# U gathers issued eighteen indices ahead of the V gathers, in place of sixteen, in a streaming encoder step

## The chip, the core and the metric

One core of one Trainium2 chip runs the whole program in one launch. The metric is the device time of an execution in microseconds (us), lower is better. The times below are of the kernel before the change; one more execution was recorded by the hardware profiler, and all rows come from that one.

## What is computed

One layer of a hybrid encoder for 1024 prompt rows and 32 sample rows of width 1024: a norm, a projection, four mLSTM heads beside eight sliding-window attention heads, an output projection, and then the part that this change touches, a product-key expert layer (PEER). For each row and each of eight heads, 16 of 16384 experts are chosen; the row is multiplied with the 16 chosen rows of the table `expert_u`, and 16 chosen rows of `expert_v` are added up with the weights that follow:

```python
idx = jnp.take_along_axis(cidx, sel, axis=-1)
g = jax.nn.softmax(top.astype(jnp.float32), axis=-1).astype(xb.dtype)
u = jnp.take(expert_u, idx, axis=0)
a = jax.nn.gelu(jnp.einsum('thkd,td->thk', u, xb), approximate=False)
ve = jnp.take(expert_v, idx, axis=0)
return jnp.einsum('thk,thkd->td', g * a, ve)
```

Everything is fp32. An expert row is 4 KB, and each (row, head) pair needs 16 of each table.

## The kernel before

The expert layer is cut into 33 subtiles of 32 rows (32 for the prompt, one for the sample), and a subtile into two groups of four heads: 66 groups (`GROUPS`). In a group the 128 partitions hold 32 rows times four heads, and `TOPK` = 16 indices follow one another. For each index one indirect DMA gathers 128 rows of `expert_u` (512 KB), another 128 rows of `expert_v`. Numbered through all groups, index n runs from 0 to 1055 in both streams; U[n] and V[n] below are these gathers. Index n = 32q + r has place r in subtile q.

**Buffers.** `ring` holds fourteen buffers, seven for U (`U_AT`) and seven for V (`V_AT`). U[n] may be gathered once VectorE is done with U[n-7] (`u_free`), V[n] once TensorE is done with V[n-7] (`v_free`).

**GpSimd** issues all gathers from one queue in one fixed order: sixteen U gathers, then pairs U[n+16], V[n] (lines 600 to 606), and at the end sixteen V gathers without partners. It waits at each gather for the free buffer (lines 581 and 593), so whatever stands behind a waiting gather waits too, of the other stream as well. The first U gather of a group also waits for the group's indices (`topk_done`).

**VectorE** takes the U stream. For U[n] it multiplies the gathered rows with the subtile's row in PSUM, `h2p`, and sums (line 1273). After a group's sixteen products ScalarE makes the gelu, and VectorE's `weigh` turns them into weights `wk` (lines 1207 to 1219); for a group in the first half of a subtile this is written behind the first product of the next group. Between the products stand pieces of the index search of a later group and the vector steps of the next tile's mixing part.

**TensorE** takes the V stream: eight matmuls for each V[n] (line 1675), weights from `wk`, sums in `acc`. Between them stand the matmuls of the next tile's mixing part and of the projection, at places that tables of numbers set. TensorE at V[t] and VectorE at U[t+16] are in the same step of these tables.

**Where the two must meet.** First, V[32q] and V[32q+16] need their group's `wk`, the former written behind product U[32q+16]. Second, `h2p` has one buffer: once in a subtile, ahead of V[32q+15], TensorE copies the rows of subtile q+1 into it (`spread_rows`, line 1628). It waits for the last product of the subtile, U[32q+31], and VectorE waits for it ahead of U[32q+32]. This handover comes 32 times in the program.

Of the kernel before, what the change touches and what calls it, by code (L numbers as in the profile page):

```python
# [28 lines left out]
PH, NK, TOPK = 8, 128, 16  # L29
# [18 lines left out]

SUB = 32
QD = D // 4  # L50
NU = 7
NV = 7
U_AT = [0, 1, 2, 3, 4, 5, 13]
# [2 lines left out]
GROUPS = 2 * (SEQ // SUB + 1)  # L56
# [119 lines left out]
def stored(b, n):  # L176

    return 16 * sum(x == b for x in UNIT_PO[:n])


def program(nc, x_prompt, x_sample, cache_k, cache_v, st_c, st_n, st_m, norm_mix_w, w_in, if_bias, mnorm_w, sinks,
# [15 lines left out]
    with ExitStack() as ctx:  # L197
        def sb(name, shape, dt=F32):
            return ctx.enter_context(nc.sbuf_tensor(name, shape, dt))

        def sem(name):
            return ctx.enter_context(nc.semaphore(name))
# [5 lines left out]
        wq_s = weights[:, DC * D:].rearrange("p (k c) -> p k c", k=DC)  # L208
        ring = sb("ring", [P, NU + NV, D])
        pj = sb("pj", [P, PJ])  # L210
# [93 lines left out]
        acc = ctx.enter_context(nc.psum_tensor("acc", [P, D], F32))  # L304
        sums = [acc[:, b * 512:b * 512 + QD] for b in range(2)]
        pbank = [acc[:, c % 2 * 512:c % 2 * 512 + PC[c][1]] for c in range(NC_)]
# [32 lines left out]
        topk_done, h2p_set = sem("topk_done"), sem("h2p_set")  # L339
        u_in = [sem(f"u_in{i}") for i in range(NU)]  # L340
        v_in = [sem(f"v_in{i}") for i in range(NV)]
# [216 lines left out]
        def _(pool):  # L558
# [16 lines left out]
            def gather_u(g, k):  # L575

                n = TOPK * g + k
                if k == 0:
                    pool.wait_ge(topk_done, g + 1)
                if n >= NU:  # L580
                    pool.wait_ge(u_free, n - NU + 1)
                elif n == 4:
                    pool.wait_ge(query_ready, 3)
                elif n == 6:
                    pool.wait_ge(proj_out[4], stored(4, len(UNITS)))
                pool.indirect_dma_start(ring[:, U_AT[n % NU], :], None, u_d,  # L586
                                        bass.IndirectOffsetOnAxis(ap=idx[:, g % 4, k:k + 1], axis=0)).then_inc(u_in[n % NU], 16)

# [8 lines left out]
                pool.indirect_dma_start(ring[:, V_AT[n % NV], :], None, v_d,  # L597
                                        bass.IndirectOffsetOnAxis(ap=idx[:, g % 4, k:k + 1], axis=0)).then_inc(v_in[n % NV], 16)

            for k in range(TOPK):  # L600
                gather_u(0, k)
            for g in range(GROUPS):
                for k in range(TOPK):
                    if g + 1 < GROUPS:
                        gather_u(g + 1, k)
                    gather_v(g, k)


# [288 lines left out]
        def _(dve):  # L897
# [330 lines left out]
            def add_rows(q):  # L1228
# [4 lines left out]
                for j in range(4):  # L1233
                    cols = slice(j * QD, (j + 1) * QD)
                    V.tensor_tensor(xt[m % 2][r, cols], xt[m % 2][r, cols], sums[q % 2][j * SUB:(j + 1) * SUB, :], ALU.add)  # L1235
# [80 lines left out]
        def _(pe):  # L1316
# [341 lines left out]
            for g in range(-1, GROUPS):  # L1658
                for k in range(TOPK):
# [5 lines left out]
                    if g >= 0 and t > 0:  # L1665
# [6 lines left out]
                        for n in (0, 1) if t == 1 else (t,):  # L1672
                            pe.wait_ge(v_in[n % NV], 16 * (n // NV + 1))
                            for j in range(4):
                                last = T.matmul(sums[g // 2 % 2][j * SUB:(j + 1) * SUB, :], wk[:, n // FEW % 5, n % FEW, :], ring[:, V_AT[n % NV], j * QD:(j + 1) * QD],  # L1675
                                                start=g % 2 == 0 and n % TOPK == 0, stop=g % 2 == 1 and k == TOPK - 1)
# [58 lines left out]
```

## Time and profile before

| what | value |
|---|---|
| median of 3 runs | 3383.86 us (3382.38 to 3389.47) |
| profiled execution | 3354.33 us |
| its span, first to last instruction | 3352.6 us |
| gathers | 2112, 512 KB each |
| mean TensorE clock granted | 0.740 |

The profile has a page of totals, a table of who waited for whom, tables of busy time in stretches of the span, and a timeline of instructions in order. Times are us from the start of the span. In all of them L586 is a U gather, L597 a V gather, L1273 a product on U, L1675 a matmul on V. A GpSimd instruction of these two lines is the making of the gather's descriptors; the transfer comes after it. `remote`, as the releaser of a wait, means that the profile did not find the instruction that ended it. In the chain that ended last, the page gives PE 31%, issue 16%, POOL 14%, DVE 13% and DMA 10%.

### The profile page before, as it was taken

What the parts mean: (1) busy time and instruction counts of PE and PEld (TensorE: products, weight loads), DVE (VectorE), ACT (ScalarE), POOL (GpSimd) and SP (SyncE); (2) the same over time, 40 slices, a digit from 0 to 9 for tenths busy, and PEclk for the clock granted to TensorE, in tenths of its full rate; (3) what the DMA queues carried; (4) which work ended last, traced back from release to release, by engine and by line L of the source; (5) the groups of instructions that cost most, each with busy time, mean ns of one, the idle gap of its engine ahead of it and who ended that gap; (6) DMA issues with size and microseconds to landing.
All of it is one profiled execution on the core that took longest, in us unless ns stands there. A gap on an engine that the chain in (4) does not pass through costs nothing.

```text
span 3352.6 us, 42363 instructions
## 1 busy us (share of the span) xinstructions
PE 2349.4 (70%) x15147; PEld 1174.5 (35%) x15147; DVE 2147.1 (64%) x5579; ACT 535.9 (16%) x1059; POOL 1992.9 (59%) x2128
## 2 busy tenths in 40 slices
PE   8995775667667888877857765668567765675545
PEld 4652352335233533334534432325223431221111
DVE  1257757776676656657577667676676676766653
ACT  2211111211121221112121111111111111210001
POOL 0036666666666566665666666666666666666665
PEclk9996796678566988987867776678676875566555
DMA  6479999999999999999999999999999999999998
GB/s 229 149 277 405 358 349 375 362 373 349 375 357 381 368 402 408 408 400 357 362 353 365 366 369 363 360 372 351 376 361 374 364 353 377 359 359 362 368 368 325
DMA packets 348955, 1197.59 MB, mean 357 GB/s; under 512 B 37760, under 2 KB 54408, under 8 KB 346952
## 3 DMA queue, kind: packets, MB, share of 16 engines
q0 software_dynamic: 304128, 1107.43, 87.8%
q1 hardware_dynamic: 44616, 87.45, 7.1%
q8 instruction: 119, 1.95, 0.2%
q14 instruction: 92, 0.75, 0.1%
HBM read 1180.69 MB, written 14.15 MB: 356 GB/s over the span
## 4 chain that ended last, share of the span: by engine, by line
PE 31%; issue 16%; POOL 14%; DVE 13%; DMA 10%; another core or an unknown queue 9%; DVEq 5%; ACT 1%; ACTq 0%; SPq 0%; POOLq 0%
PE mx L1574 9%; PE acc L1675 7%; POOL ring L597 7%; POOL ring L586 7%; DVE ring L1273 6%; DMA ring<-in_peer_v_dram,idx 4%; PE mx L1385 3%; DMA ring<-in_peer_u_dram,idx 3%; DVEq L1145 2%; PE acc L1361 2%; PE mx L1585 2%; PE mx L1556 1%; DMA weights<-in_w_in_dram 1%; PE h2p L1628 1%
## 5 line engine op out<-in xcount | busy, mean ns | idle before, releaser
L1273 DVE SCALAR_TENSOR_TENSOR ring<-ring,h2p 128x1024 f32<-128x1024 f32 x1056 | 1272.2, 1214 | 551.7 <-DMA ring<-in_peer_u_dram,idx 267.5
L1675 PE MATMUL acc<-ring,wk 128*32 128x256 f32 x8448 | 1030.7, 507 | 684.6 <-DMA ring<-in_peer_v_dram,idx 317.5
L597 POOL DMA_INDIRECT ring<-in_peer_v_dram,idx x1056 | 995.3, 942 | 790.6 <-remote 369.4
L586 POOL DMA_INDIRECT ring<-in_peer_u_dram,idx x1056 | 995.8, 943 | 554.7 <-issue 302.4
L1675 PEld LDWEIGHTS acc<-ring,wk 128*32 128x32 f32 x8448 | 316.5, 129 | 1316.5 <-issue 776.9
L1574 PE MATMUL mx<-reg,weights 128*128 128x128 f32 x1792 | 275.3, 309 | 42.4 <-issue 42.1
L1574 PEld LDWEIGHTS mx<-reg,weights 128*128 128x128 f32 x1792 | 245.8, 216 | 101.5 <-issue 101.1
L1556 PE MATMUL mx<-weights,reg 128*128 128x512 f32 (+1 forms) x256 | 138.6, 668 | 1.9 <-DVEq L1246 1.1
L1385 PE MATMUL mx<-weights 128*128 128x512 f32 (+1 forms) x288 | 132.4, 604 | 2.2 <-issue 1.4
L1628 PE MATMUL h2p<-ch,ident 32*32 32x512 f32 x528 | 104.4, 798 | 31.2 <-issue 20.2
L828 ACT ACTIVATE gl<-dots 128x16 f32<-128x16 f32 x66 | 14.2, 216 | 537.8 <-issue 368.5
L1585 PE MATMUL mx<-kT,pj 128*32 128x128 f32 x1040 | 69.5, 316 | 36.0 <-issue 30.7
L788 ACT COPY pj<-mx 128x512 f32<-128x512 f32 x32 | 18.7, 586 | 446.2 <-PE mx L1574 234.7
L1273 DVE DVE_READ_ACCUMULATOR ring<-ring,h2p 128x1 f32 x1056 | 86.8, 82 | 0.0
L828 ACT ACT_TABLE_LOAD x66 | 84.7, 1283 | 7.1 <-issue 1.7
L822 ACT ACT_TABLE_LOAD x61 | 78.3, 1283 | 44.2 <-issue 20.8
L1385 PEld LDWEIGHTS mx<-weights 128*128 128x128 f32 x288 | 55.6, 204 | 67.7 <-issue 61.2
L1235 DVE TENSOR_TENSOR xt<-xt,acc 32x256 f32<-32x256 f32 x132 | 55.1, 417 | 24.0 <-PE acc L1675 21.9
L1556 PEld LDWEIGHTS mx<-weights,reg 128*128 128x128 f32 (+1 forms) x256 | 45.5, 196 | 69.1 <-issue 66.7
L1219 DVE TENSOR_TENSOR wk<-rept,gl 128x128 f32<-128x128 f32 x264 | 65.5, 289 | 5.8 <-issue 0.5
L1585 PEld LDWEIGHTS mx<-kT,pj 128*32 128x32 f32 x1040 | 49.9, 125 | 54.6 <-issue 48.8
L1385 PE MATMUL mx<-weights,reg 128*128 128x512 f32 (+1 forms) x96 | 49.8, 670 | 22.6 <-DMA weights<-in_w_in_dram 18.4
(311 smaller groups left out, 2425.6 us busy)
## 6 DMA issues: line engine op xcount, KB each, us to landing
ring<-in_peer_u_dram,idx POOLq DMA_INDIRECT x1056
ring<-in_peer_v_dram,idx POOLq DMA_INDIRECT x1056
weights<-in_peer_w_q_dram SPq DMA_DIRECT2D x7, 2048.0 KB
weights<-in_w_in_dram SPq DMA_DIRECT2D x5, 2048.0 KB, 18.2
weights<-in_w_in_dram SPq DMA_DIRECT2D x10, 1024.0 KB
ring<-in_peer_w_q_dram SPq DMA_DIRECT2D x8, 1024.0 KB, 6.1
xt<-in_x_prompt_dram SPq DMA_DIRECT2D x8, 512.0 KB
ring<-in_w_out_dram SPq DMA_DIRECT2D x2, 2048.0 KB, 13.6
```

The costliest lines, as they stand in the source:

```text
L586: pool.indirect_dma_start(ring[:, U_AT[n % NU], :], None, u_d, bass.IndirectOffsetOnAxis(ap=idx[:, g % 4, k:k + 1], axis=0)).then_inc(u_in ...
L597: pool.indirect_dma_start(ring[:, V_AT[n % NV], :], None, v_d, bass.IndirectOffsetOnAxis(ap=idx[:, g % 4, k:k + 1], axis=0)).then_inc(v_in ...
L822: S.activation(ew[:, :], top[:, g % 3, :], ACT.Exp, bias=ntop[:, g % 3:g % 3 + 1], accum_out=ez[:, 0:1])
L828: S.activation(gl[:, :], dots[:, g % 2, :], ACT.Gelu)
L1145: dve.drain()
L1273: V.scalar_tensor_tensor(ring[:, U_AT[n % NU], :], ring[:, U_AT[n % NU], :], 1.0, h2p[:, :], ALU.mult, ALU.mult, accum_out=dots[:, (g + 1) ...
L1385: last = T.matmul(bank, hT1_again[i][:, 4 * half + k, :], wpiece[(2 * p + half) % 3][:, k, 0:w], start=half + k == 0, stop=half == 1 and k ...
L1556: last = T.matmul(mx[0:n, 2 + half, :], t8[:, k, 0:n], w, start=k == 0, stop=k == DC - 1)
L1574: last = T.matmul(mx[:, i // 4, i % 4 * P:i % 4 * P + n], w, t8[:, k, 0:n], start=k == 0, stop=k == DC - 1)
L1585: last = T.matmul(mx[q:q + SUB, i, col:col + NK], qT[:, c, i * SUB:(i + 1) * SUB], kT[:, c % 2, :], start=True, stop=True)
L1628: last = T.matmul(h2p[j * SUB:(j + 1) * SUB, cols], ident[r, r], ch[m % 2][r, cols], start=True, stop=True)
L1675: last = T.matmul(sums[g // 2 % 2][j * SUB:(j + 1) * SUB, :], wk[:, n // FEW % 5, n % FEW, :], ring[:, V_AT[n % NV], j * QD:(j + 1) * QD], ...
```

## The change

The lead of the U stream over the V stream in GpSimd's order becomes a constant, `U_AHEAD = 18`. Eighteen U gathers go first, then pairs U[n+18], V[n], and the last eighteen V gathers have no partner. The waits of each gather are the same as before, and so are the buffers and the programs of all other engines.

```diff
+U_AHEAD = 18
...
-            for k in range(TOPK):
-                gather_u(0, k)
+            for n in range(U_AHEAD):
+                gather_u(n // TOPK, n % TOPK)
             for g in range(GROUPS):
                 for k in range(TOPK):
-                    if g + 1 < GROUPS:
-                        gather_u(g + 1, k)
+                    n = TOPK * g + k + U_AHEAD
+                    if n < TOPK * GROUPS:
+                        gather_u(n // TOPK, n % TOPK)
                     gather_v(g, k)
```

GpSimd's queue at the first V gather, before: the rows are U[7] to U[15], U[16], V[0], U[17], V[1]; `topk_done` is the wait for the next group's indices.

```order
L586 DMA ring<-in_peer_u_dram,idx 128x1024 [waits u_free] x9
L586 DMA ring<-in_peer_u_dram,idx 128x1024 [waits u_free,topk_done]
L597 DMA ring<-in_peer_v_dram,idx 128x1024
L586 DMA ring<-in_peer_u_dram,idx 128x1024 [waits u_free]
L597 DMA ring<-in_peer_v_dram,idx 128x1024
```

The same place in the changed kernel, whose lines are one further down:

```order
L587 DMA ring<-in_peer_u_dram,idx 128x1024 [waits u_free] x9
L587 DMA ring<-in_peer_u_dram,idx 128x1024 [waits u_free,topk_done]
L587 DMA ring<-in_peer_u_dram,idx 128x1024 [waits u_free] x2
L598 DMA ring<-in_peer_v_dram,idx 128x1024
L587 DMA ring<-in_peer_u_dram,idx 128x1024 [waits u_free]
L598 DMA ring<-in_peer_v_dram,idx 128x1024
```

U[17] and U[18] have moved ahead of V[0], so V[0] has two gathers more in front of it, and from there on each V[n] stands right behind U[n+18].

GpSimd's queue at the end, before:

```order
L597 DMA ring<-in_peer_v_dram,idx 128x1024
L586 DMA ring<-in_peer_u_dram,idx 128x1024
L597 DMA ring<-in_peer_v_dram,idx 128x1024
L586 DMA ring<-in_peer_u_dram,idx 128x1024
L597 DMA ring<-in_peer_v_dram,idx 128x1024 x17
```

and in the changed kernel:

```order
L598 DMA ring<-in_peer_v_dram,idx 128x1024
L587 DMA ring<-in_peer_u_dram,idx 128x1024
L598 DMA ring<-in_peer_v_dram,idx 128x1024
L587 DMA ring<-in_peer_u_dram,idx 128x1024
L598 DMA ring<-in_peer_v_dram,idx 128x1024 x19
```

The last U gather now stands ahead of V[1037] where it stood ahead of V[1039]: nineteen V gathers follow it in place of seventeen.

## Rows read from the trace of the kernel before

**Rows 1.** The page: busy time of the engines, then the gathers' DMA queue.

```profile
PE 2349.4 (70%) x15147; PEld 1174.5 (35%) x15147; DVE 2147.1 (64%) x5579; ACT 535.9 (16%) x1059; POOL 1992.9 (59%) x2128
...
q0 software_dynamic: 304128, 1107.43, 87.8%
```

**Rows 2.** Table by stretch: length, busy us of engines, granted clock, DMA share, GB/s.

```profile
1200.00:1400.00 200.00, 163.03 (x863) 67.13 (x864) 126.24 (x327) 27.48 (x42) 127.13 (x135) 0.91 1.03 407
...
3000.00:3200.00 200.00, 110.04 (x726) 33.85 (x725) 133.43 (x347) 21.17 (x34) 130.67 (x139) 0.63 0.98 364
```

**Rows 3.** Waits of GpSimd: who waited for whom, us, times, longest.

```profile
POOL ring L597 <- remote: 369.4, 201, 3.6
...
POOL ring L597 <- PE acc L1675: 181.1, 127, 6.7
POOL ring L586 <- DVE ring L1273: 62.0, 79, 9.7
```

**Rows 4.** Waits of TensorE and VectorE at V and U, same table.

```profile
PE acc L1675 <- DMA ring<-in_peer_v_dram,idx: 317.5, 184, 7.9
...
DVE ring L1273 <- DMA ring<-in_peer_u_dram,idx: 267.5, 185, 4.8
...
DVE ring L1273 <- PE h2p L1628: 72.2, 12, 15.2
...
PE acc L1675 <- DVEq L1215: 51.6, 12, 10.8
```

**Rows 5.** Timeline of GpSimd at one handover: start, us, instruction, idle before.

```profile
3143.73 0.94 POOL L597 DMA_INDIRECT ring<-in_peer_v_dram,idx  x1 [0.30 <-issue]
3144.97 0.94 POOL L586 DMA_INDIRECT ring<-in_peer_u_dram,idx  x1 [0.30 <-issue]
3146.22 0.94 POOL L597 DMA_INDIRECT ring<-in_peer_v_dram,idx  x1 [0.30 <-issue]
...
3151.50 0.93 POOL L597 DMA_INDIRECT ring<-in_peer_v_dram,idx  x1 [3.10 <-PE acc L1675]
```

**Rows 6.** VectorE at the same handover: the first product of the new subtile.

```profile
3151.17 1.22 DVE L1273 SCALAR_TENSOR_TENSOR ring<-ring,h2p 128x1024 f32<-128x1024 f32 x1 [11.77 <-remote]
```

**Rows 7.** TensorE behind the same handover.

```profile
3151.07 4.09 PE L1675 MATMUL acc<-ring,wk 128*32 128x256 f32 x40 [0.39 <-issue]
3156.16 0.64 PE L1675 MATMUL acc<-ring,wk 128*32 128x256 f32 x8 [1.00 <-DMA ring<-in_peer_v_dram,idx]
```

**Rows 8.** Timeline of GpSimd at an earlier handover.

```profile
2961.36 0.94 POOL L597 DMA_INDIRECT ring<-in_peer_v_dram,idx  x1 [1.97 <-PE acc L1675]
```

**Rows 9.** VectorE at that earlier handover.

```profile
2964.69 1.22 DVE L1273 SCALAR_TENSOR_TENSOR ring<-ring,h2p 128x1024 f32<-128x1024 f32 x1 [2.74 <-PE h2p L1628]
2965.84 0.08 DVE L1273 DVE_READ_ACCUMULATOR ring<-ring,h2p 128x1 f32 x1
```

**Rows 10.** TensorE at a V gather whose weights come late.

```profile
2258.96 1.08 PE L1675 MATMUL acc<-ring,wk 128*32 128x256 f32 x8 [10.75 <-DVEq L1215]
```

**Rows 11.** VectorE ahead of those weights.

```profile
2242.07 1.22 DVE L1273 SCALAR_TENSOR_TENSOR ring<-ring,h2p 128x1024 f32<-128x1024 f32 x1
...
2254.30 0.69 DVE L1123 COPY reg<-mx 128x512 f32<-128x512 f32 x1 [11.01 <-remote]
2255.11 1.22 DVE L1273 SCALAR_TENSOR_TENSOR ring<-ring,h2p 128x1024 f32<-128x1024 f32 x1
```

**Rows 12.** Timeline of GpSimd at the start: V[0], V[4], V[5].

```profile
228.67 0.93 POOL L597 DMA_INDIRECT ring<-in_peer_v_dram,idx  x1 [0.30 <-issue]
...
241.76 0.94 POOL L597 DMA_INDIRECT ring<-in_peer_v_dram,idx  x1 [3.47 <-DMA proj_scratch<-ring]
...
250.95 0.94 POOL L597 DMA_INDIRECT ring<-in_peer_v_dram,idx  x1 [7.00 <-DMA proj_scratch<-ring]
```

**Rows 13.** Timeline at the start and the end: first matmul on V, last V gather.

```profile
247.76 1.93 PE L1675 MATMUL acc<-ring,wk 128*32 128x256 f32 x32
...
3338.08 0.93 POOL L597 DMA_INDIRECT ring<-in_peer_v_dram,idx  x1 [0.30 <-issue]
```

## The prediction, made before the changed kernel ran

> **What bounds the kernel now.** I read the page first. No engine is full: TensorE is busy for 70% of the span, VectorE for 64%, GpSimd for 59%, and the gathers' DMA queue fills 87.8% of sixteen engines [rows 1]. The table by stretch says more about the DMA: its share is 0.98 in a late stretch at 364 GB/s, but in another stretch, at a similar share, it moves 407 GB/s [rows 2]. So a share near one is not the queue at its best rate; there is about a tenth left, and it is lost somewhere in the supply of gathers.
>
> The timeline of GpSimd shows the supply. Where nothing holds it, a gather goes out every 1.24 us (3144.97 less 3143.73) [rows 5]. 2112 gathers at 1.24 us are 2619 us. From the first V gather at 228.67 [rows 12] to the last at 3338.08 [rows 13] pass 3109 us. What GpSimd waits for is in its table of waits: 369.4 + 181.1 = 550.5 us ahead of V gathers, in 328 waits, and 62.0 us ahead of U gathers, in 79 waits [rows 3]. Of each wait some 0.3 us is there in any case, as between any two gathers. The V waits carry two names, `remote` and the matmul on V; both are the wait for a free V buffer, since no other wait stands in the code there after the first seven. So the fixed order of the two streams is mostly held by TensorE, and hardly ever by VectorE.
>
> Last I read what the two consumers wait for [rows 4]. TensorE waits 184 times, 317.5 us, for a V gather to land; VectorE 185 times, 267.5 us, for a U gather. TensorE waits 12 times, 51.6 us, for weights, and VectorE 12 times, 72.2 us, for the new rows in `h2p`.
>
> **What the change does.** It adds and removes no instruction: 1056 gathers of each kind go out before and after, with the same waits. It moves each U gather two places ahead in relation to the V gathers, which is two pairs, 4 x 1.24 = 5.0 us where nothing holds the queue. Only waits can change.
>
> *Gain in the middle.* When GpSimd stands at V[n] for a free buffer, two more U gathers are already out. VectorE may then go on for two products more. That is worth something only where TensorE then waits for VectorE. There are 12 such waits for weights, 51.6 us [rows 4]. The one I looked into is the longest: TensorE idles 10.75 us until 2258.96 [rows 10]. In that time VectorE has done a product at 2242.07, then stood 11.01 us, and the instruction that it stood at is the copy of the next tile's transposed rows, which TensorE makes [rows 11]. Its next product starts at 2255.11 without any idle time for a landing. So VectorE was late for the weights because of the mixing part, not because of U. I take the gain here at nothing; its bounds are zero and 51.6 us.
>
> *Cost at the handover.* At the handover VectorE has finished U[32q+31] and TensorE is at V[32q+15]. The seven U buffers allow U[32q+38] and no more until the product on U[32q+32] is done. Before, V[32q+21] and V[32q+22] stand ahead of U[32q+39] in the queue, so V[32q+21] goes out during the pause, and V[32q+22] as soon as TensorE is done with V[32q+15]. After the change U[32q+39] stands ahead of V[32q+21], so that V gather, and all behind it, wait for VectorE. Two handovers show the price. In the first, V[32q+21] went out at 3146.22 [rows 5]; VectorE's first product of the new subtile starts at 3151.17 and takes 1.22 us [rows 6], so U[32q+39] would go out at 3152.4 and V[32q+21] at 3153.6, later by 7.4 us. TensorE had its next buffers at 3151.07, did forty matmuls, five indices, and was waiting for a landing at 3156.16 already [rows 7]; here the delay is paid. In the second, V[32q+21] went out at 2961.36 [rows 8], VectorE's product ended at 2965.92 [rows 9], so it would go out at 2967.2, later by 5.8 us. The least it can be is two places in the queue, 2.5 us, where VectorE resumes at once. I take 5 us, between these: 32 x 5 = 160 us of delay of V gathers.
>
> How much of it lies on the path? TensorE waited for the landing of 184 of its 1056 V gathers, 0.17 [rows 4]; the others had landed before. 160 x 0.17 = 27 us. Of this a part goes into the following wait for weights, where TensorE would have stood anyway: 12 waits against 32 handovers, so 12/32 is taken off, which leaves 17 us. The bounds are zero, if the buffers always hide it, and 160 us.
>
> *Elsewhere in a subtile.* V[n] now also needs VectorE done with U[n+11], before U[n+9]. The U waits of before, 62.0 us, show how seldom that held [rows 3]; two indices more will hold more often. The nearest row is that one, and doubling it, with the same 0.17 on the path, gives 62 x 0.17 = 11 us; the lower bound is zero. Against it stands the same amount of earlier U gathers for VectorE, which waits for them as often (185 times) but for which TensorE seldom waits. I leave both out of the sum and keep 11 us for the range.
>
> *Start and end.* V[0] goes out 2.5 us later than at 228.67, behind two more U gathers, but TensorE has its first matmul on V at 247.76 [rows 13], behind projection work, so this costs nothing. V[4] and V[5] wait 3.47 and 7.00 us for stores out of the ring [rows 12]; the two additional U gathers go out in that time. From there on the program has two gathers fewer to issue between the V gathers, and at the end eighteen V gathers run alone in place of sixteen. If GpSimd sets the end, that is 2 x 1.24 = 2.5 us less; bounds 0 and 2.5. I take 2.5.
>
> *The sum*, on the profiled execution: 3354.3 + 17 - 2.5 = 3368.8 us. That execution is 29.5 us below the median of the runs shown, so I add the difference to the median: 3383.9 + 14.5 = 3398 us, 0.4% slower.
>
> **The rivals.** *Faster.* Two thirds and more of GpSimd's waits come ahead of V gathers [rows 3], so a lead that lets more U out in that time evens the two streams. It decides if VectorE's 185 waits for U [rows 4] push the handover or the weights later. Against it speak rows 10 and 11, for it that in late stretches TensorE has little mixing work and is busy for 110 of 200 us [rows 2]. Price: half of the 51.6 us of waits for weights, and the 2.5 us: 3383.9 - 28 = 3356 us.
>
> *No change.* The gathers are the same, in one queue, and the queue is nearly always busy. If the transfers set the pace, a gather that is late here is made up by the next wait for a buffer, and only the 2.5 us at the end remain: 3381 us, within 0.2%. For it speaks the DMA share of 0.98, against it the 407 GB/s at another time [rows 2]. The wait that returns in each subtile at the V ring, with only seven buffers, would by this view stay as it is. The Trainium skill ("Perfetto Trace Analysis", Optimization Strategy) says that a gap that keeps repeating on the engine that should be full can mean too few buffers; by that rule the order of the gathers would not help, and the time would be this one.
>
> *The change does less than it says.* Where both rings are full the rings, not the order, decide what goes out next, and U cannot be eighteen ahead. The result is that of no change, and I count it there.
>
> *Slower by more.* If most handovers are like the first of the two, where TensorE is out of V gathers 5 us after it resumes, 32 x 5 = 160 us are paid to more than a third: about 60 us, 3441 us.
>
> The Trainium skill ("DMA: Bandwidth & Descriptors", Anatomy of one DMA) gives a transfer issued by GpSimd as about 2.0 us plus its bytes at 436 GB/s, so 3.2 us for 512 KB as an estimate, and says that the fixed part is latency of completion. By it a buffer that is freed comes back no sooner than 3.2 us later, and a V gather that goes out 5 us late is missed more surely than the factor 0.17 has it. No row here shows the whole of one transfer, and the sum does not use it.
>
> **How the numbers follow.** Slower by 5 to 30 us, the sum above, 0.33; slower by more, 0.12; no change, 0.28; faster, 0.27. A measurement of this kernel can tell about 0.2%, 7 us, from no change. So slower 0.45, same 0.28, faster 0.27. The forecast is 3398 us. The range for 8 in 10 leaves out the far half of "slower by more" and the far part of "faster": 3350 to 3445 us. The likeliest case alone has 3388 to 3415 us.
>
> **What would show it.** If I am right, the profile after has U waits (line 587) of 150 us and more in place of 62.0, the largest just behind each handover, V waits (line 598) well below 550 us, and more of TensorE's time waiting for V to land than 317.5 us. If the faster rival is right, TensorE's waits for weights and VectorE's for U landings fall and the wait for V landings does not rise. If nothing changes, the sum of GpSimd's waits stays at 613 us and only moves from V to U. The forecast is wrong if V gathers behind a handover go out late and TensorE still has landed buffers, or if the product on U[32q+32] is not what holds GpSimd there.

## The result, and the profile after

| | kernel before | changed kernel |
|---|---|---|
| median, us | 3383.12 (4 runs, 3381.24 to 3389.47) | 3480.40 (4 runs, 3472.04 to 3484.11) |
| ratio | 1 | 1.0278, 95% interval 1.0264 to 1.0292 |
| profiled execution, us | 3354.3 (span 3352.6) | 3481.21 (span 3479.5) |

The changed kernel is slower by 2.8%, 97 us on the medians. The profiled executions differ by 126.9 us. The forecast was 3398 us with a range up to 3445: the direction is right, the size is not, and the result lies outside the range.

The page of the changed kernel, to be read beside [rows 1]:

```profile
PE 2379.1 (68%) x15147; PEld 1179.8 (34%) x15147; DVE 2141.1 (62%) x5579; ACT 536.1 (15%) x1059; POOL 1992.5 (57%) x2128
...
q0 software_dynamic: 304128, 1107.43, 85.5%
```

Instructions, bytes and GpSimd's busy time are what they were. TensorE's busy time rises by 29.7 us, at a mean granted clock of 0.729 in place of 0.740; it does not follow the cost, since a kernel shown below that costs 7.2% has it at 2380.0 us. The rest is waits. Their table shows them (who waited for whom: us, times, longest; U gathers are line 587, V gathers 598, the matmul on V 1677, the product 1275, the weights 1217):

```profile
PE acc L1677 <- DMA ring<-in_peer_v_dram,idx: 425.3, 238, 7.1
POOL ring L587 <- DVE ring L1275: 317.2, 159, 10.9
POOL ring L598 <- remote: 315.6, 170, 3.5
...
DVE ring L1275 <- DMA ring<-in_peer_u_dram,idx: 207.7, 127, 4.8
...
DVE ring L1275 <- PE h2p L1630: 124.5, 18, 16.1
...
POOL ring L598 <- PE acc L1677: 114.3, 117, 3.8
...
PE acc L1677 <- DVEq L1217: 64.6, 11, 13.6
```

Against [rows 3] the waits ahead of U gathers went from 62.0 to 317.2 us, and those ahead of V gathers fell from 550.5 to 315.6 + 114.3 = 429.9 us; the sum rose from 612.5 to 747.1, by 134.6 us. Against [rows 4] TensorE waits 107.8 us more for V to land and 13.0 us more for weights. These two are 120.8 us of the 126.9, though such a sum isn't exact: what TensorE waits for in one place it may have waited for elsewhere. VectorE waits 59.8 us less for U to land. So it did get its U earlier, as the change would have it; but it waits 52.3 us more for the new rows in `h2p` (72.2 to 124.5), and nothing came of it.

The chain of work that ended last, by engine, in the kernel before and then in the changed kernel:

```profile
PE 31%; issue 16%; POOL 14%; DVE 13%; DMA 10%; another core or an unknown queue 9%; DVEq 5%; ACT 1%; ACTq 0%; SPq 0%; POOLq 0%
```

```profile
PE 31%; DVE 19%; issue 16%; another core or an unknown queue 10%; DMA 8%; POOL 8%; DVEq 7%; ACT 1%; SPq 0%; ACTq 0%; POOLq 0%
```

GpSimd's share fell from 14% to 8% and VectorE's rose from 13% to 19%. Before, the end was set in good part by the stream of gathers; now VectorE's steps, with the gathers that wait for them, have taken that place.

The table by stretch (length, busy us of PE, PEld, DVE, ACT, POOL, granted clock, DMA share, GB/s) tells it for the queue. First nearly the whole of the streams and one stretch of the kernel before, then of the changed one:

```profile
1600.00:1800.00 200.00, 131.74 (x1062) 82.52 (x1063) 134.84 (x356) 36.36 (x75) 124.21 (x133) 0.74 0.96 357
...
230.00:3330.00 3100.00, 2123.39 (x14102) 1045.10 (x14100) 2080.72 (x5385) 482.94 (x948) 1968.07 (x2088) 0.72 0.98 370
```

```profile
1600.00:1800.00 200.00, 148.01 (x1090) 90.47 (x1082) 126.23 (x330) 29.29 (x58) 112.65 (x120) 0.76 0.90 326
...
230.00:3330.00 3100.00, 2086.04 (x13691) 1032.06 (x13689) 2016.18 (x5272) 471.91 (x928) 1885.25 (x2000) 0.72 0.95 355
```

In these 3100 us GpSimd has 2000 instructions in place of 2088, and the rate falls from 370 to 355 GB/s at the same granted clock, 0.72.

**One handover.** GpSimd, VectorE and TensorE of the changed kernel, each from its timeline:

```profile
3079.53 0.94 POOL L598 DMA_INDIRECT ring<-in_peer_v_dram,idx  x1 [0.31 <-issue]
3086.07 0.94 POOL L587 DMA_INDIRECT ring<-in_peer_u_dram,idx  x1 [5.60 <-DVE ring L1275]
3087.32 0.94 POOL L598 DMA_INDIRECT ring<-in_peer_v_dram,idx  x1 [0.30 <-PE acc L1677]
```

```profile
3084.57 1.22 DVE L1275 SCALAR_TENSOR_TENSOR ring<-ring,h2p 128x1024 f32<-128x1024 f32 x1 [6.19 <-PE h2p L1630]
```

```profile
3088.17 2.79 PE L1677 MATMUL acc<-ring,wk 128*32 128x256 f32 x24
3093.31 1.08 PE L1677 MATMUL acc<-ring,wk 128*32 128x256 f32 x8 [2.35 <-DMA ring<-in_peer_v_dram,idx]
```

The gather that waits 5.60 us is U[935], place 7 of its subtile, for the first product on the new rows. Behind it V[917] goes out at 3087.32. Had nothing held the queue, U[935] would have taken the next slot, at 3080.77, and V[917] the one after it, at 3082.01: it is 5.3 us late. Its own buffer was free at 3079.03, when the matmuls on V[910] ended, so the order alone held it. TensorE works off the buffers that have landed and then idles 2.35 us for this very gather. This is the mechanism that the prediction described, and here of the size that it took, 5 us.

**One place off the handover.** This is what it had left out of its sum:

```profile
3035.78 0.93 POOL L598 DMA_INDIRECT ring<-in_peer_v_dram,idx  x1 [0.30 <-issue]
3040.31 0.93 POOL L587 DMA_INDIRECT ring<-in_peer_u_dram,idx  x1 [3.59 <-DVE ring L1275]
3041.54 0.93 POOL L598 DMA_INDIRECT ring<-in_peer_v_dram,idx  x1 [0.30 <-issue]
3043.45 0.93 POOL L587 DMA_INDIRECT ring<-in_peer_u_dram,idx  x1 [0.98 <-DVE ring L1275]
```

```profile
3038.09 0.81 DVE L1086 TENSOR_REDUCE s<-mx 32x4 f32<-32x640 f32 x1 [2.54 <-remote]
3038.83 1.20 DVE L1275 SCALAR_TENSOR_TENSOR ring<-ring,h2p 128x1024 f32<-128x1024 f32 x1
...
3041.97 1.20 DVE L1275 SCALAR_TENSOR_TENSOR ring<-ring,h2p 128x1024 f32<-128x1024 f32 x1
```

```profile
3041.97 1.08 PE L1677 MATMUL acc<-ring,wk 128*32 128x256 f32 x8 [1.92 <-DMA ring<-in_peer_v_dram,idx]
3046.70 1.08 PE L1677 MATMUL acc<-ring,wk 128*32 128x256 f32 x8 [3.65 <-DMA ring<-in_peer_v_dram,idx]
3050.09 1.08 PE L1677 MATMUL acc<-ring,wk 128*32 128x256 f32 x8 [2.31 <-DMA ring<-in_peer_v_dram,idx]
```

VectorE stands 2.54 us at a step of the mixing part, then makes the product on U[914] (3038.83). U[921] needs that product's buffer and waits 3.59 us, and V[903] stands behind it. While V[903] is held, TensorE runs out of landed V: it ends V[901] at 3040.05, V[902], the last one out, is still in flight, and its matmul starts after 1.92 us of idle time. V[903] then costs 3.65 us. So a hitch of VectorE in the middle of a subtile is paid by TensorE, and nothing here has to do with a handover.

Places 21 to 24 of a subtile are those of the V gathers just behind the handover. Adding up TensorE's waits for landings ahead of the first matmul of each V index, by place, shows that both kinds are there:

| kernel (the last two are explained below) | places 21 to 24, us | all other places, us |
|---|---|---|
| before | 37.1 | 280.4 |
| changed | 90.3 | 335.0 |
| at_handover | 65.5 | 278.3 |
| off_handover | 26.7 | 337.7 |

Half of the new waits of the changed kernel lie just behind the handovers (53.2 us), half elsewhere (54.6 us). Not every handover is paid at once: V[32q+21] or V[32q+22] is waited for behind 12 of 32 handovers, behind 6 before.

### The profile page after: what moved, and what is told of

It is laid out like the page before. It is cut to its first block, busy times and chain, and to the rows that moved or that the text cites. A ratio compares the mean times of both kernels' runs of the same rounds, so it can differ in the third digit from the quotient of the medians.

```text
span 3479.5 us, 42363 instructions
## 1 busy us (share of the span) xinstructions
PE 2379.1 (68%) x15147; PEld 1179.8 (34%) x15147; DVE 2141.1 (62%) x5579; ACT 536.1 (15%) x1059; POOL 1992.5 (57%) x2128
## 4 chain that ended last, share of the span: by engine, by line
PE 31%; DVE 19%; issue 16%; another core or an unknown queue 10%; DMA 8%; POOL 8%; DVEq 7%; ACT 1%; SPq 0%; ACTq 0%; POOLq 0%
DVE ring L1275 9%; PE mx L1576 9%; PE acc L1677 7%; DMA ring<-in_peer_v_dram,idx 5%; POOL ring L598 4%; POOL ring L587 4%; DVEq L1147 4%; PE acc L1363 2%; PE mx L1387 2%; PE h2p L1630 2%; DMA ring<-in_peer_u_dram,idx 2%; PE mx L1587 2%; PE mx L1558 2%; PE acc L1348 1%
## 5 line engine op out<-in xcount | busy, mean ns | idle before, releaser
L1677 PE MATMUL acc<-ring,wk 128*32 128x256 f32 x8448 | 1036.9, 514 | 776.0 <-DMA ring<-in_peer_v_dram,idx 425.3
L587 POOL DMA_INDIRECT ring<-in_peer_u_dram,idx x1056 | 997.2, 944 | 794.6 <-DVE ring L1275 317.2
L598 POOL DMA_INDIRECT ring<-in_peer_v_dram,idx x1056 | 993.5, 941 | 677.4 <-remote 315.6
L1630 PE MATMUL h2p<-ch,ident 32*32 32x512 f32 x528 | 119.6, 806 | 28.9 <-issue 23.9
L1209 DVE RECIPROCAL ez<-ez 128x1 f32<-128x1 f32 x66 | 10.6, 161 | 120.1 <-ACTq L831 60.8
```

The costliest lines, as they stand in the source:

```text
L1630: last = T.matmul(h2p[j * SUB:(j + 1) * SUB, cols], ident[r, r], ch[m % 2][r, cols], start=True, stop=True)
```

## The experiments

All of them keep the gathers and the arithmetic and set only the order of the two streams or the number of buffers, and with the latter which earlier product or matmul a gather waits for. Those that set the order replace the issue loop by

```
u = 0
for n in range(TOPK * GROUPS):
    while u < min(TOPK * GROUPS, n + lead(n) + 1):
        gather_u(u // TOPK, u % TOPK)
        u += 1
    gather_v(n // TOPK, n % TOPK)
```

`lead(n)` of 16 gives the order of the kernel before, of 18 that of the change. The lead and the number of U buffers, NU, together say which product a V gather depends on. Ahead of V[n] stands U[n+lead], and that needs the product on U[n+lead-NU]. I call lead less NU the **distance**: 9 before, 11 after the change. Nine is a special value here. V[n] also needs the matmuls on V[n-7], and by the program's tables these stand in the same step as the product on U[n+9]. At distance nine both conditions fall due in the same step; at eleven V[n] waits for the step of V[n-5], as if the V ring had five buffers in place of seven.

The runs were made on several chips, and the same kernel takes different times on them: the kernel before took 3388.33 us beside the first four runs, 3360.57 and 3357.26 us beside others, and 3111.61 to 3112.70 us beside seven of them. Each ratio is against the kernel before on the same chip at the same time. I call the last kind of chip the quick one. The waits in the tables are of one profiled execution each; those of the kernel before are from the profile shown above.

### Handover or elsewhere: the change split by place

`off_handover` has lead 18, but lets V[32q+21] and V[32q+22] go ahead of U[32q+39], as before. `at_handover` is its opposite: the order of before but for that place.

```
-    return 16
+    return {21: 17, 22: 16, 23: 16, 24: 17}.get(n % 32, 18)                    # off_handover
+    return {19: 17, 20: 18, 21: 18, 22: 18, 23: 18, 24: 17}.get(n % 32, 16)    # at_handover
+    return 17                                                                  # lead17
+    return 15                                                                  # lead15
```

> Edit: the lead is 18 everywhere, except that V[32q+21] and V[32q+22] go out ahead of U[32q+39] (lead 17, 16, 16, 17 at places 21 to 24 of a subtile, 18 again from place 25 on). Theory H, the handover makes the cost: in the changed kernel U[32q+39] waits behind the handover for 110 us in 32 handovers, V[32q+21] behind it, and that alone is the 97 us. Then this kernel is back at 3383 us within 0.5%, 3370 to 3400 us. Theory G, the cost is general: each V[n] now waits for the product on U[n+11], at any place. Then most stays: 3435 to 3475 us, with the U waits at places other than 39 as in the changed kernel, some 190 us.

> Edit: the reverse part alone. The lead is 16 everywhere, except 17, 18, 18, 18, 18, 17 at places 19 to 24 of a subtile, so that U[32q+39] stands ahead of V[32q+21] and V[32q+22] as in the changed kernel, and nowhere else is anything moved. Theory H: 3450 to 3480 us, as slow as the changed kernel, with about 110 us of U waits at that place. Theory G: 3383 to 3415 us, since only two of 32 V gathers come late, and they have landed neighbours.

> Edit: a lead of 17 everywhere. At a handover both rings then fill at the same pair: V[32q+21] still goes out in the pause, U[32q+39] is ahead of V[32q+22] alone. Theory H: nearly all of the cost is gone, 3383 to 3405 us. Theory G, each V[n] waits for the product on U[n+10]: about a third to half of the cost, 3410 to 3435 us.

> Edit: a lead of 15 everywhere, the other direction. At a handover V[32q+22] stands ahead of U[32q+38], so one U gather fewer is out when the V ring is full. Theory H says nothing of it but that the handover cost is nil: 3375 to 3400 us. Theory G, in which V gathers freed of the U ring are worth time: 3365 to 3383 us, unless VectorE then runs out of U gathers, in which case it is slower, 3390 us and more, with TensorE's waits for weights above 52 us.

Measured, with the waits in us (times):

| kernel | ratio, 95% interval | U gathers for VectorE | V gathers, both names | TensorE for V landings |
|---|---|---|---|---|
| lead15 | 1.0020, 1.0008 to 1.0033 | 39.4 (72) | 634.8 | 271.0 (162) |
| before | 1 | 62.0 (79) | 550.5 | 317.5 (184) |
| lead17 | 1.0078, 1.0056 to 1.0099 | 153.3 (132) | 524.5 | 333.9 (199) |
| at_handover | 1.0123, 1.0100 to 1.0145 | 158.9 (100) | 527.4 | 343.9 (195) |
| off_handover | 1.0216, 1.0192 to 1.0240 | 194.4 (145) | 529.7 | 366.0 (208) |
| changed | 1.0278, 1.0264 to 1.0292 | 317.2 (159) | 429.9 | 425.3 (238) |

The rows of off_handover that carry the verdict:

```profile
PE acc L1678 <- DMA ring<-in_peer_v_dram,idx: 366.0, 208, 7.0
...
POOL ring L601 <- PE acc L1678: 198.1, 155, 6.0
POOL ring L590 <- DVE ring L1276: 194.4, 145, 10.5
```

Neither of the two explanations holds alone. The handover alone costs 1.2%, some 42 us of 3388; everything but the handover costs 2.2%, 73 us. Each half has its new waits of TensorE where the edit put them (the table by place above): at_handover 28.4 us more at places 21 to 24 and none elsewhere, off_handover 57.3 us more elsewhere and none at these places. Together they are more than the whole (3.4 against 2.8%), so the two costs do not simply add; where they overlap is not shown. The larger part is the one that the prediction left out of its sum. Lead seventeen, one place, costs less than a third of two places. Lead fifteen is no better than sixteen: TensorE waits 46 us less for V, VectorE 355.1 us for U in place of 267.5. Its waits for weights, 49.3 us, did not rise above 52 us, as was expected of the slower case.

### Where VectorE mixes, or everywhere

VectorE's mixing steps lie in some groups only. `mix_only` has off_handover's order where they are (87 of 128 indices), `no_mix_only` where they are not.

```
+    return H(n) if n % 128 >= 72 or n % 128 < 31 else 16     # mix_only, H as in off_handover
+    return 16 if n % 128 >= 72 or n % 128 < 31 else H(n)     # no_mix_only
```

They ran first on a quick chip, with two kernels that have one U buffer fewer:

> Edit: lead 18 (with the handover left as before, as in off_handover) only at the 87 of 128 indices of a tile at which VectorE has steps of the next tile's mixing part between its products; lead 16 at the other 41. off_handover as a whole costs 2.16%. Theory S, the cost is made where VectorE stands still for the mixing part: a full U ring then stops the queue, V gathers with it, and TensorE, on whose matmuls VectorE waits, runs out of V. Then this kernel has nearly all of it, 1.019 to 1.022, 3450 to 3460 us. Theory E, the cost is even, by indices: 87/128 of it, 1.0147, 3435 us.

> Edit: the counterpart of mix_only, lead 18 (the handover left as before) only at the 41 of 128 indices without mixing steps on VectorE, 16 elsewhere. Theory S: 0.998 to 1.003, 3380 to 3395 us, perhaps faster than the kernel before, since U gathers that go out early there cost nothing. Theory E: 41/128 of 2.16%, 1.007, 3409 us.

Measured there: mix_only 1.0029 (1.0020 to 1.0039), no_mix_only 1.0027 (1.0015 to 1.0040). The loss nearly vanished with the chip, so they were run again on a chip of the first kind, with the changed kernel beside them:

> The changed kernel once more, beside the next two. The last four kernels ran on a chip on which the kernel before takes 3113 us in place of 3388: GpSimd's waits ahead of V gathers all have TensorE as releaser there, none is `remote`, the gathers move 409 GB/s, and TensorE is busy 2152 us in place of 2349. Theory T: the cost of the lead is made where TensorE itself is slow at times, as in the kernel before at 3142 to 3151 us, where it starts one matmul per 0.7 us. On a chip like the first (before near 3385 us): 1.026 to 1.030. On one like the second (before near 3113 us): at most 1.006, as the transfers set the pace. Against T: about 1.02 and more on either.

> mix_only again, with the changed kernel beside it. If the kernel before takes about 3385 us on this chip, theory S (cost only where VectorE has mixing steps) expects 1.019 to 1.022, theory E (cost even by indices) 1.0147. If it takes about 3113 us: 1.003, as measured there.

> no_mix_only again. If the kernel before takes about 3385 us on this chip, theory S expects 0.998 to 1.003, theory E 1.007. If it takes about 3113 us: 1.003, as measured there.

Measured: lead18 1.0276 (1.0257 to 1.0295), which repeats the result beside a kernel before of 3360.57 us; mix_only_b 1.0102 (1.0078 to 1.0127); no_mix_only_b 1.0074 (1.0056 to 1.0092). That the cost sits in the mixing steps alone is wrong: without any of them it is 0.7%, in 41 of 128 indices. An even spread of off_handover's 2.2% would be 1.5 and 0.7%; the second is met, the first is somewhat below. The example above shows a mixing step as the cause of one wait; which of VectorE's other steps (the top-k of the coming group, the weights) make the rest was not looked into. These two kernels also show that TensorE's waits for landings are no measure of the cost: they are 437.0 us in mix_only_b, more than the 425.3 us of the changed kernel, at 1.0% in place of 2.8%.

### Order or distance: one U buffer fewer

With six U buffers at lead sixteen the order of the queue is that of before and the distance that of lead seventeen. At lead fifteen the distance is that of before.

```
-NU = 7
+NU = 6
-        ring = sb("ring", [P, NU + NV, D])
+        ring = sb("ring", [P, 14, D])
+    return 15          # six_u_15 only
```

On the quick chip:

> Edit: the kernel before, lead 16, but only six of the seven U buffers are used. V[n] stands behind U[n+16], which now waits for the product on U[n+10] (before: U[n+9], in the changed kernel: U[n+11]), as in lead17. Theory D, what counts is how far back the product lies on which V[n] depends, lead less buffers: at least the 0.8% of lead17, 3410 to 3430 us, with some 150 us of U waits. Theory L, what counts is the lead itself, how much of the queue is U: like the kernel before or little above, 3385 to 3400 us.

> Edit: lead 15 and six U buffers. The product on which V[n] depends is U[n+9] again, as in the kernel before; VectorE has one gather fewer to draw on. Theory D: back to the time of lead15, 3385 to 3405 us, faster than six_u although a U gather fewer is out. Theory L: slower than six_u, 3400 us and more, since both the lead and the buffers are smaller.

Measured: six_u 1.0012 (1.0002 to 1.0021), six_u_15 1.0023 (1.0013 to 1.0032). There the distance of ten costs 0.1%, so this pair could not settle the question. On a chip of the first kind, with the changed kernel and a lead of twenty:

> Lead sixteen, as before, but six U buffers in place of seven. V[n] then stands behind a U gather that needs the product on U[n+10], as with lead seventeen and seven buffers. Theory D (what costs is the distance from a V gather to the product that it indirectly needs, lead less U buffers) expects about what lead seventeen cost beside the kernel before, 1.006 to 1.010. Theory L (the order of the queue itself costs, by what lands late) expects 1.002 or less, since the order is as before. A ratio well above 1.010 would say that fewer U buffers cost by themselves.

> Lead fifteen and six U buffers: V[n] needs the product on U[n+9], exactly as in the kernel before. Theory D expects 1.000 to 1.004, below six U buffers at lead sixteen; theory L expects at least what lead fifteen gave with seven buffers, 1.002, and nothing in favour of it over lead sixteen.

> Lead twenty, seven U buffers: V[n] needs the product on U[n+13]. Lead 16, 17 and 18 gave 1.000, 1.008 and 1.028. Theory D, with a cost that grows faster than the distance, expects 1.06 to 1.10, with more than 500 us of waits ahead of U gathers and V waits below 250 us. If the cost were a single loss at each handover that is used up once the order is turned round there, it would level off, at 1.03 to 1.04.

> The changed kernel again (lead eighteen, seven U buffers), on whatever chip this call gets. If the chip is one on which the kernel before takes 3360 to 3390 us, both theories expect the ratio of before, 1.026 to 1.030. If it is one on which the kernel before takes about 3113 us: theory T (the coupling of V[n] to the product on U[n+11] costs only where TensorE goes through stretches of one instruction pair per 0.70 us) expects 1.006 or less, since the two halves cost 1.0029 and 1.0027 there; a cost that belongs to the order alone would be 1.02 or more.

| kernel | distance | ratio, 95% interval | U gathers for VectorE | TensorE for V landings |
|---|---|---|---|---|
| six_u_15_b | 9 | 1.0011, 1.0001 to 1.0021 | 83.7 (93) | 254.4 (151) |
| six_u_b | 10 | 1.0129, 1.0110 to 1.0147 | 157.9 (109) | 364.5 (200) |
| lead18_c | 11 | 1.0245, 1.0226 to 1.0263 | 284.4 (140) | 400.1 (229) |
| lead20 | 13 | 1.0718, 1.0694 to 1.0743 | 553.1 (218) | 696.1 (357) |

First six_u_b, then lead20, from their waits:

```profile
PE acc L1675 <- DMA ring<-in_peer_v_dram,idx: 364.5, 200, 6.7
POOL ring L597 <- remote: 352.7, 195, 3.5
...
POOL ring L586 <- DVE ring L1273: 157.9, 109, 9.7
```

```profile
PE acc L1678 <- DMA ring<-in_peer_v_dram,idx: 696.1, 357, 7.6
POOL ring L590 <- DVE ring L1276: 553.1, 218, 14.0
```

The order of before with one U buffer fewer costs 1.3%. With the lead taken back by one as well, at the old distance, the same six buffers cost 0.1%. So at distance nine a U buffer is worth next to nothing by itself, and most of what costs is the distance. Not all is settled: six_u_b is above lead seventeen (1.0129 against 1.0078, intervals apart), and its expectation had named a ratio well above 1.010 as the sign that a buffer fewer costs by itself. The two were not run side by side, and the changed kernel itself gave 1.0276 and 1.0245 beside two sets of runs of the kernel before, the latter below its expected range, so it stays open whether that half per cent is the buffer's. Lead twenty goes on as distance has it: 7.2%, 553.1 us of waits ahead of U. Its waits ahead of V, 304.8 us, stayed above the 250 us that were expected as a limit. A loss paid at the handovers alone was expected to level off at 3 to 4%.

The traces allow a closer look at what the distance takes away. For each V gather, at the end of its GpSimd instruction, count the V buffers that are taken: the gathers issued whose matmuls have not ended, this one included. The mean over indices 20 to 1019, for the first kind of chip:

| kernel | distance | cost | V buffers taken, mean |
|---|---|---|---|
| six_u_15_b | 9 | 0.1% | 4.74 |
| before | 9 | 0 | 4.71 |
| lead15 | 8 | 0.2% | 4.69 |
| no_mix_only_b | 9 to 11 | 0.7% | 4.59 |
| lead17 | 10 | 0.8% | 4.50 |
| mix_only_b | 9 to 11 | 1.0% | 4.49 |
| six_u_b | 10 | 1.3% | 4.49 |
| at_handover | 9 to 11 | 1.2% | 4.48 |
| off_handover | 9 to 11 | 2.2% | 4.45 |
| changed, three profiles | 11 | 2.4 to 2.8% | 4.25 to 4.27 |
| lead20 | 13 | 7.2% | 3.64 |

Nearly throughout, this number falls where the cost rises, which TensorE's waits do not; off_handover alone costs clearly more than its place in the list suggests. That fits a distance above nine working like a smaller V ring, though a count that goes along with the cost doesn't prove it. By the same view a distance of eight adds nothing, since there the seven V buffers themselves are the nearer limit, and in lead15 it does add nothing.

### A V buffer in the freed place

If distance is what counts, the U buffer can be given to V, and the lead kept at fifteen or less. This was the attempt at a kernel better than both. Besides these edits, the first V gather into the new eighth buffer waits, at the start, for the stores out of that buffer.

```
-NU = 7
-NV = 7
-V_AT = [6, 7, 8, 9, 10, 11, 12]
+NU = 6
+NV = 8
+V_AT = [6, 7, 8, 9, 10, 11, 12, 13]
+    return 15          # eight_v_15
+    return 14          # eight_v_14
```

> The free slot goes to the V side: six U buffers, eight V buffers, lead fifteen. V[n] needs the product on U[n+9] as in the kernel before, and the matmul on V[n-8] in place of V[n-7]. Theory D (only the distance to the product that a V gather needs costs, and what is bought with a buffer is TensorE's reserve of landed V) expects at least the ratio of six U buffers at lead fifteen, 1.001, and less if the reserve helps: 0.992 to 1.000, with TensorE's waits for landings of V under 250 us. The rival, that the supply is bound by the transfers themselves and a buffer more only moves the wait, expects 1.000 to 1.003.

> As the other, at lead fourteen: V[n] needs the product on U[n+8], one step less far than in the kernel before. Theory D in its simple form (nearer is never worse for V) expects TensorE's waits for landings of V to fall again and the time to be that of lead fifteen within 0.3%; what it can lose is that U arrives late for the weights, which lead fifteen with seven buffers showed as more waits of VectorE for landings: 1.002 to 1.008 if that decides.

> The kernel with six U and eight V buffers at lead fifteen once more, which ran on a chip where the kernel before takes 3112 us and gave 1.0007 there. On a chip where it takes 3350 to 3390 us: if the reserve of landed V absorbs TensorE's and VectorE's uneven steps, 0.992 to 0.999 and waits for landings of V under 240 us; if the reserve does not decide at the distance of before, 1.000 to 1.003. On a chip of the other kind: 1.0007 again, within 0.001.

Measured: eight_v_15 1.0007 (0.9997 to 1.0017) and, on another chip, 1.0007 again (0.9998 to 1.0016); eight_v_14 1.0028 (1.0019 to 1.0038). The gain that was hoped for (0.992 to 1.000, with V waits of TensorE under 250 us) did not come; in eight_v_15 these waits are 616.0 us. All three ran on quick chips, though, so whether the reserve helps where the change costs most stays open. On the quick chip it does not. For eight_v_15 the reason lies partly in the order: V[n-8] stands in the step of U[n+8], but at distance nine V[n] still waits for U[n+9], so the eighth buffer can seldom be used. All eight are taken at 85 of the 1000 gathers of indices 20 to 1019, in eight_v_14 at 180. The waits show why a nearer distance does not pay either: in eight_v_14 TensorE waits 452.6 us for V to land, less than in eight_v_15, and 265.1 us for weights in place of 188.8. What it gains on the one side it begins to lose on the other. That VectorE, which makes the weights, gets its U later there is the likely reason, but was not shown. No kernel tried is faster than the kernel before.

### The two kinds of chip

The page of mix_only on a quick chip, to be read beside [rows 1]:

```profile
PE 2152.2 (69%) x15147; PEld 1046.5 (34%) x15147; DVE 2151.1 (69%) x5579; ACT 535.9 (17%) x1059; POOL 1995.2 (64%) x2128
```

and the waits of its gathers:

```profile
POOL ring L590 <- DVE ring L1276: 228.0, 273, 7.0
POOL ring L601 <- PE acc L1678: 194.1, 247, 6.7
```

VectorE, ScalarE and GpSimd are busy as long as on the other chips; TensorE is busy 2152 us in place of 2349, at nearly the same granted clock (0.730 and 0.740 over the span). Not one V gather waits for `remote` there, where the kernel before on the other kind has 201 such waits. One thing that differs can be seen in TensorE's weight loads of the kernel before, on the first kind of chip, at the handover of [rows 5] to [rows 7]:

```profile
3148.27 0.13 PEld L1675 LDWEIGHTS acc<-ring,wk 128*32 128x32 f32 x1 [1.27 <-issue]
3148.98 0.13 PEld L1675 LDWEIGHTS acc<-ring,wk 128*32 128x32 f32 x1 [0.59 <-issue]
3149.67 0.13 PEld L1675 LDWEIGHTS acc<-ring,wk 128*32 128x32 f32 x1 [0.57 <-issue]
3150.37 0.13 PEld L1675 LDWEIGHTS acc<-ring,wk 128*32 128x32 f32 x1 [0.57 <-issue]
```

For some seven microseconds TensorE starts one weight load with its matmul per 0.70 or 1.40 us, and waits for nothing that the profile shows. Weight loads that start 0.66 to 0.74 us after the one before are 228 in the kernel before and 228 in the changed one; in mix_only on the quick chip they are 18. I have no cause for them. That they are why the kinds differ in what the change costs was argued and not isolated: where TensorE itself moves unevenly, a V gather that hangs on VectorE too may find the reserve empty more often. The count of taken V buffers fits: 5.38 on the quick chip in mix_only and 5.40 in six_u, in place of 4.49 in both on the other kind. On the quick chip the queue moves 400 GB/s nearly throughout (230 to 3080 us of mix_only, at a share of 1.02), and DMA is 36% of the chain of work that ended last, in place of 10% in the kernel before on the other kind. So there the transfers largely set the pace, and a short hold of the queue costs little. The changed kernel as a whole was not run on a quick chip; the two parts of off_handover, mix_only and no_mix_only, cost 0.3% each there.

## Why the prediction was wrong, point by point

**What bounds the kernel.** Right in its main reading: no engine is full, and the supply of gathers carries the end. TensorE was taken as the one that holds the gathers, VectorE as one that hardly ever does. That held for the kernel before and was taken for slack, and that was the mistake: 62.0 us of U waits said how often distance nine is short, not how near to short it is the rest of the time. The prediction wrote down that V[n] would need U[n+11], but not that the V ring's own limit, V[n-7], stands in the step of U[n+9], so that nothing was left to give.

**Gain in the middle, taken at nothing.** Right. VectorE's waits for U to land fell by 59.8 us and TensorE's waits for weights did not fall (51.6 to 64.6).

**Cost at the handover, 17 us.** The mechanism was right and the place too. Adding up, over the whole timeline, the idle time ahead of the U gathers at place 7, less the 0.30 us that is there in any case, gives 3 us in 2 waits before and 110 us in 31 waits after. The 160 us of the sum were too many by half, since the stall is 3.5 us on average and not five. What was mis-sized more is the share on the path. The handover alone cost 42 us where its 159 us of U waits are 97 more than before: a share of 0.43, in place of 17 of 160, 0.11. The 0.17 behind it had been taken from how often TensorE waits for a V at all, over the whole run. It is a mean over all V gathers, most of which go out on time. Those behind a held U gather go out late in a row, and in the two examples TensorE uses up its landed buffers meanwhile; that this makes the share larger is my reading of them, not a measurement. Nor was there ground to take off 12/32 for waits for weights: these were 51.0 us in at_handover, as before (51.6).

**Elsewhere in a subtile, 11 us, kept out of the sum.** This is the step that failed most. It took the waits of 62.0 us and doubled them. In off_handover they rose to 194.4, by 132 us, and cost 73 us: a share of 0.55. So the term is 73 us in place of 11, by twice as much waiting and three times the share on the path. The doubling had no row behind it. Two places more of distance take away two products' time from the slack of every U gather of the run, and how many of them had less slack than that isn't shown by the waits that stick out. The series of leads, with seven U buffers, shows it: U waits of 39.4, 62.0, 153.3, 317.2 and 553.1 us for distances 8, 9, 10, 11 and 13.

**Start and end, a gain of 2.5 us.** Nothing came of it. V[0] goes out at 229.81 in place of 228.67 [rows 12], later by 1.1 us and not 2.5. The first matmul on V starts at 246.42 in place of 247.76 [rows 13], and the last V gather goes out 15.0 us ahead of the end of the span in place of 14.5 (3352.6 less 3338.08).

**The rivals.** *Faster* and *no change* are out: TensorE's wait for V rose, and GpSimd's waits did not keep their sum of 613 us but rose to 747. The rule of the Trainium skill that stood with the second ("Perfetto Trace Analysis", Optimization Strategy), that a recurring gap may mean too few buffers, doesn't fit the U side: six buffers at distance nine cost 0.1%, whereas seven at distance eleven cost 2.8%. On the V side one buffer more gave 1.0007, on the quick chip alone and in an order that seldom lets it be used, so the rule is not refuted for V; that a larger distance works like a smaller V ring speaks for it. *The change does less than it says* is out too: VectorE's products are on average 16.8 indices ahead of TensorE's in the changed kernel, in place of 16.0, and the waits moved. *Slower by more*, 3441 us, was given 0.12 and comes closest, but by the handovers alone, and these cost 42 us by themselves, not 60.

**The signs.** U waits of 150 us and more with the largest just behind the handovers (place 7 has 119.4 of the 317.2 us), V waits well below 550 us and longer waits of TensorE for V were all found, so they showed the mechanism. They had no upper ends, and so couldn't tell 15 us from 97. The direction was forecast from the handover alone, at 0.45, and came out for that reason and for a second one that the sum did not hold.

**The range.** Measured by themselves the two terms are 42 and 73 us, 115 in sum, of which the whole change shows 97; the sum had 17 and 0. The range was too narrow mainly because the least known term got the narrowest bounds, 0 and 11 us, as the nearest row was small; and the upper end of 3445 us left no room for the handovers' own bound of 160 us.

## What to carry to other kernels

Where one queue feeds two consumers in a fixed order, write down for each gather which product and which matmul it hangs on, directly and through the gather ahead of it; lead less buffers is the number to look at, not the lead, and it is to be held against the step in which the other ring frees its buffer (here nine): beyond it, the second ring had fewer buffers taken here, as if it were smaller. Waits that are small in the trace say that a limit is seldom reached, not how far away it is, so a change that moves every item nearer to such a limit has to be priced by the spread of the consumer's steps, with a wide upper end. Of the time for which a stream is held up in short pieces, the whole paid a far larger share here (0.43 and 0.55) than the share of gathers that its consumer waited for before (0.17).

## What was not expected of the hardware

The same kernel took 3357 to 3388 us on some chips and 3112 us on others, 8 to 9% apart, more than anything tried here. On the first kind TensorE goes through stretches in which it starts an instruction per 0.70 us or per twice that, at no wait that the profile shows (weight loads 0.66 to 0.74 us behind the one before: 228 in the kernel before, 11 to 24 in each of the seven runs on quick chips). The price of the change went with it: 2.8, 2.8 and 2.4% on the first kind, 0.3% for each of the two parts of off_handover on the other.

The time from the issue of a gather to its use is also longer than the 3.2 us that the prediction worked out from the Trainium skill ("DMA: Bandwidth & Descriptors", Anatomy of one DMA). V[903] goes out at 3041.54 and TensorE, which waits for it, starts at 3046.70: 5.2 us, and for V[917] it is 6.0 us. The page gives its figure per DMA, and no row here shows one gather by itself: other gathers are in flight at the same time.

That the second place costs more than twice the first (0.8% for lead seventeen, 2.4 to 2.8% for eighteen, 7.2% for twenty) was measured. The mean of taken V buffers falls along with it (4.71, 4.50, 4.25 and 3.64 for leads sixteen, seventeen, eighteen and twenty); why the cost rises faster than that is open.
